# First layer of a two-block model: the keys' scale on ScalarE, and a new order of key transposes, first scores and value pairs

## The chip, the cores and the metric

The kernel runs on one core of one Trainium2 chip. The metric is the device time of one execution in microseconds (us): the median of several executions. A core has five engines with a queue each, worked off in order: TensorE (matmuls), VectorE, ScalarE, GpSimd and SyncE (which here only issues DMAs). Engines wait for one another by semaphores. In the profile they are called PE (PEld is TensorE's loading of the stationary operand), DVE, ACT, POOL and SP.

## The reference

A sequence of 256 tokens of width 1024 goes through two layers of a first block and one layer of a second, in float32. Only the mixer of the first layer is touched here. It projects the normed input and splits it in parts for a state-space mixer, a gated unit and differential attention:

```python
xn = rms_norm(h, attn_norm_g[layer])
proj = xn @ w_in[layer]
u_ssm, u_g, v_g, q, k, v = jnp.split(proj, [o1, o2, o3, o4, o5], axis=-1)
...
q = rms_norm(q, q_gain)          # 4 heads x 2 halves of 64
k = rms_norm(k, k_gain)
q = apply_rope(q, cos, sin)
k = apply_rope(k, cos, sin)
...
s = jnp.einsum("bqhcd,bkhcd->bhcqk", qb, k).astype(jnp.float32) * scale
s = jnp.where(mask, s, -jnp.inf)
p = jax.nn.softmax(s, axis=-1)
w = (p[:, :, 0] - lam * p[:, :, 1]).astype(v.dtype)
return jnp.einsum("bhqk,bkhe->bqhe", w, v)
```

The norm of a key is one factor for each token and each of the 8 half heads. The kernel turns the keys first and multiplies by that factor (held in `hr[:, 1, 8 * t + g]`, token tile t, half head g) afterwards: this multiplication is the keys' scale.

## The kernel before

**Weights.** All weights come in a stream of pairs of 128x1024 float32, 512 KB each. SyncE loads a pair into one of 7 raw buffers. ScalarE copies it to a rounded high part (`hi_upto`, line 1065, 6 buffers), VectorE subtracts to get a low part (`lo_upto`, line 1644, 7 buffers), and TensorE makes three products for each (high by high, high by low, low by high; lines 575 to 577 in `pair_products`). `hi_upto(n)` and `lo_upto(n)` do all pairs below n that aren't done yet; they stand by hand between the other work of their engine, which fixes the order. A high part waits until TensorE has used the pair 6 before it, a low part waits for its high part, and TensorE waits for both.

In layer 0 the pairs are numbered: q 0 to 3, k 4 to 7, state-space input 8 and 9, gates (`gmlp0`) 10 to 13, v 14 to 17, and then the output projection. The 256 tokens are two tiles of 128, so the three products of a pair make 12 matmuls (2 blocks of 128 rows, 2 tiles).

**TensorE in the stretch that the change touches** (lines 823 to 853), in layer 0: the transposes of the turned queries, the state-space input's shuffle and products (`input_products`), gate pairs 10 and 11, the transposes of the scaled keys (`head_transposes(1, ...)`, line 727), gate pairs 12 and 13, the scores of batch 0 (`scores(0)`: a mask product, line 741, and 16 small ones, line 744), v pairs 14 and 15, the Toeplitz products (line 650), v pair 16, the scores of batch 1, the spatial gating's products, v pair 17, the transposes of batch 0's probabilities, the scores of batch 2, and then the state-space output products (`output_products`, line 686).

**VectorE there**, layer 0: turns the keys (`rotary`), prepares the phase table (lines 341 to 343), low part 12, the keys' scale (line 1854, one operation over 128x1024), a memset (line 1858), low part 13, the rotation of the state-space inputs (`rotate`, lines 1781, 1782, 1785, 1786: two products from PSUM with a table, two sums), low part 14, the row maxima of the scores of batch 0 (`batch_max(0)`, lines 1796 and 1799), the small `lambdas`, low parts 15 and 16, the scans (line 1871), low part 17, `gate_rows`, `combine(0)`, low part 18, `states`, low part 19, and `batch_max(1)`.

**ScalarE there**, layer 0: high parts 15 and 16, the phase tables (lines 352 to 357), copies of the transposed keys out of PSUM (lines 1174, 1175), high part 17, the gates' squares (line 1182), high part 18, the exponentials of batch 0 (line 1207), the Toeplitz blocks' copies (line 1109), high part 19, the exponentials of batch 1, high part 20, the copy of the transposed probabilities (line 1215).

**GpSimd there**: the keys' inverse root (lines 1472, 1473, semaphore `hr_ready`), then six products of 128x1024 for the state-space output powers (lines 383 to 385, twice).

Of the kernel before, what the change touches and what calls it, by code (L numbers as in the profile page):

```python
# [21 lines left out]
TOK, TT = 256, 2  # L22
# [4 lines left out]
QKD, VD, DH = 64, 128, 4  # L27
# [11 lines left out]
ALU, ACT, AX = mybir.AluOpType, mybir.ActivationFunctionType, mybir.AxisListType  # L39
# [97 lines left out]
def build(nc, weights, x, mem, cols, rows, lams, bmerge, consts, amask, bexp, cexp, wst, wglu, out):  # L137
    with ExitStack() as ctx:
# [5 lines left out]
        def sem(name):  # L144
            if name not in sems:
                sems[name] = ctx.enter_context(nc.semaphore(name))
            return sems[name]
# [51 lines left out]
        def wide(ap, n, dim=1):  # L199

            a = ap.unsqueeze(dim)
            shape = list(a.shape)
            shape[dim] = n
            return a.to_broadcast(shape)
# [140 lines left out]
        def phase_tables(act, l):  # L345

            f, k = phase_scratch(l)
            co, si = (etab[:, i, :, :].rearrange("p s c -> p (s c)") for i in range(2))
            act.wait_ge(sem("turns_ready"), l + 1)
            if l:  # L350
                act.wait_ge(sem("states_ready"), 2 * l)
            act.activation(k, f, ACT.Sin, scale=-3.1415925).then_inc(sem("etab_ready"), 1)
            act.activation(si, f, ACT.Sin, scale=-6.283185).then_inc(sem("etab_ready"), 1)
            act.wait_ge(sem("etab_ready"), 4 * l + 1)
            act.activation(k, k, ACT.Square, scale=math.sqrt(2.0)).then_inc(sem("etab_ready"), 1)
            act.wait_ge(sem("etab_ready"), 4 * l + 3)
            act.activation(co, k, ACT.Identity, scale=-1.0, bias=1.0).then_inc(sem("etab_ready"), 1)
# [156 lines left out]
        def _(pe):  # L514
# [67 lines left out]
            def project(name, fm=False, xh=xth, xl=xtl, ready=None, pairs=None, order=None, half=None):  # L582

                c = chunk(name)
                _, n_k, cw = CHUNKS[c]
                banks = [PJ[BUF[c]][:, 0, :], PJ[BUF[c]][:, 1, :]]
                per = 1024 // cw
                for j in (range(PAIRS[c]) if pairs is None else pairs):  # L590
                    if j == 0:
                        emptied(name)
                    if ready:
                        pe.wait_ge(ready[0], ready[1] + (j + 1) * ready[2])
                    m = pair_products(SLOT[name, j], (order[j] if order else j) * per, banks, fm, xh, xl, cw,
                                      j == 0, j == PAIRS[c] - 1, half)
                    m.then_inc(pair_used, 1)
# [58 lines left out]
            for l in range(LAYERS):  # L656
# [61 lines left out]
                def head_transposes(which, banks):  # L718

                    if which == 0:  # L720
                        pe.wait_ge(sem("q_rot"), 2 * (l + 1))
                    else:
                        pe.wait_ge(sem("k_scaled"), l + 1)
                    for h in range(DH):
                        for t in range(TT):
                            o = banks[h // 2][:, (h % 2) * TOK + t * P:(h % 2) * TOK + (t + 1) * P]
                            m = pe.transpose(o, xn[:, t, which * 512 + h * P:which * 512 + (h + 1) * P], ident)
                    m.then_inc(sem("qk_tr"), 1)

                def scores(b):  # L730

                    t, heads = DB[b]
                    n = P * (t + 1)
                    if b == 0:
                        pe.wait_ge(sem("qk_ev"), 4 * (l + 1))
                    if b == 1:
                        pe.wait_ge(sem("w_used"), 2 * (l + 1))
                    if b == 2:
                        pe.wait_ge(sem("da_exp"), 16 * l + EXPS[0])
                    for c, bank in enumerate(DBANKS[b]):  # L740
                        pe.matmul(bank[:, :], identb[:, :], maskb[:, t, :], start=True, stop=False, skip_group_check=True)
                    for i, h in enumerate(heads):
                        for c, bank in enumerate(DBANKS[b]):
                            m = pe.matmul(bank[:, i * n:(i + 1) * n], qT[c * QKD:(c + 1) * QKD, h, t * P:(t + 1) * P],
                                          kT[c * QKD:(c + 1) * QKD, h, 0:n], start=False, stop=True, skip_group_check=True)
                    m.then_inc(sem("da_sc"), 1)
# [81 lines left out]
                if l == 0:  # L828
                    shuffle_in()
                    input_products()  # L830
                    project("gmlp0", pairs=[0, 1])
                    head_transposes(1, (S0, S1))
                else:
                    project(f"gmlp{l}", pairs=[0])
                    shuffle_in()
                    project(f"gmlp{l}", pairs=[1])
                    head_transposes(1, (S0, S1))
                    input_products()
                project(f"gmlp{l}", pairs=[2, 3])
                if l == 0:  # L840
                    pe.wait_ge(sem("maskb_ready"), 3)
                scores(0)
                if l == 0:
                    project("v0", pairs=[0, 1])
                    pe.wait_ge(sem("w_used"), 2)
                    for b in range(2):
                        toeplitz_products(0, b, (T0, T1)[b])
                    project("v0", pairs=[2])
                    pe.wait_ge(sem("mt_ready"), 8)
                    scores(1)  # L850
                    sgu_products()
                    project("v0", pairs=[3])
                    prob_transposes(0)
                else:
                    project(f"v{l}", pairs=[0])
                    scores(1)
                    project(f"v{l}", pairs=[1])
                    sgu_products()
                    project(f"v{l}", pairs=[2])
                    prob_transposes(0)  # L860
                    project(f"v{l}", pairs=[3])
# [193 lines left out]
        def _(act):  # L1055
# [81 lines left out]
            for l in range(LAYERS):  # L1137
# [32 lines left out]
                hi_upto(s0 + 17)  # L1170
                if l == 0:
                    phase_tables(act, 0)
                act.wait_ge(sem("qk_tr"), 2 * l + 2)
                act.copy(kT[:, 0:2, :], S0[:, :]).then_inc(sem("qk_ev"), 1)
                act.copy(kT[:, 2:4, :], S1[:, :]).then_inc(sem("qk_ev"), 1)
# [452 lines left out]
        def _(dve):  # L1628
# [122 lines left out]
            for l in range(LAYERS):  # L1751
# [6 lines left out]
                def heads8(ap):  # L1758
                    return ap.rearrange("p t (g d) -> p t g d", g=8)
# [89 lines left out]
                if l == 0:  # L1849
                    phase_turns(dve, link, 0)  # L1850
                    lo_upto(s0 + 13)
                dve.wait_ge(sem("hr_ready"), 2 * l + 2)
                k8 = heads8(xn[:, :, 512:1024])
                dve.tensor_tensor(k8, k8, wide(hr[:, 1, :].rearrange("p (t g) -> p t g", t=TT), QKD, 3), ALU.mult)\
                   .then_inc(sem("k_scaled"), 1)
                if l == 0:
                    dve.wait_ge(sem("mixw_landed"), 32)
                    dve.memset(wsts[64:128, :, 0:64], 0.0).then_inc(sem("wst_ready"), 1)
# [29 lines left out]
                if l:  # L1888
                    lo_upto(s0 + 18)
                    scans()  # L1890
                    batch_max(0)
                    lo_upto(s0 + 19)
                    gate_rows()
                    states()
                    lo_upto(s0 + 20)
                    dve.wait_ge(sem("states_ready"), 2 * (l + 1))
                    combine(0)
                    batch_max(1)
                else:
                    lo_upto(s0 + 15)  # L1900
                    batch_max(0)
                    lambdas()
                    lo_upto(s0 + 17)
                    scans()
                    lo_upto(s0 + 18)
                    gate_rows()
                    dve.wait_ge(sem("par_a"), 6)
                    for k in range(LAYERS):
                        link(dve.tensor_tensor(nlam[:, k:k + 1], lamv[:, 6 + k:7 + k], lamv[:, 2 + k:3 + k], ALU.subtract))
                        link(dve.tensor_scalar(nlam[:, k:k + 1], nlam[:, k:k + 1], -LAMBDA_INIT[k], None, ALU.add))  # L1910
                    combine(0)
                    lo_upto(s0 + 19)
                    states()
                    lo_upto(s0 + 20)
                    batch_max(1)
                    dve.wait_ge(sem("states_ready"), 2)
                    for k in range(LAYERS):
                        link(dve.tensor_scalar(row("sub", VD * k, VD), row("sub", VD * k, VD), math.sqrt(VD) * (1.0 - LAMBDA_INIT[k]),
                                               None, ALU.mult))
# [416 lines left out]
```

## Time and profile before

| | |
|---|---|
| Median of 3 executions | 1042.14 us (1041.73 to 1047.3) |
| The profiled execution | 1040.72 us, span 1038.9 us |
| TensorE busy | 1000.9 us (96%), 6106 matmuls |
| VectorE busy | 695.3 us (67%) |
| ScalarE busy | 547.9 us (53%) |
| GpSimd busy | 246.6 us (24%) |
| Mean granted clock of TensorE | 0.997 of full |

The span is the time from the first to the last recorded instruction; the execution's own time is 1.8 us longer. The busy shares are means over the whole program; the change touches the stretch from about 50 to 100 us of it. Times in the rows below are counted from the span's start. In the timelines a row is one instruction or several alike (x4), with its start and its duration; in brackets stands how long the engine was idle before it and what it waited for.

### The profile page before, as it was taken

How to read it: one execution, taken by the hardware profiler on the slowest of the kernel's cores; microseconds unless marked ns; L12 is line 12 of the kernel's file. 1: busy time of each engine (PE TensorE's matmuls, PEld its weight loads, DVE VectorE, ACT ScalarE, POOL GpSimd, SP SyncE). 2: the span in 40 equal slices, each digit the busy share in tenths (PEclk: the TensorE clock that was granted, in tenths of full speed). 3: DMA queues.
4: the chain of work that ended last, by engine and by line, in shares of the span. 5: the costliest groups of instructions: out<-in, count | busy, mean ns of one | idle time of the engine just before them, and what ended most of it. 6: DMA issues, size and time to landing. Idle time of an engine off the chain costs nothing.

```text
span 1038.9 us, 15870 instructions
## 1 busy us (share of the span) xinstructions
PE 1000.9 (96%) x6106; PEld 871.1 (84%) x6110; DVE 695.3 (67%) x1084; ACT 547.9 (53%) x910; POOL 246.6 (24%) x196
## 2 busy tenths in 40 slices
PE   5979999999999999999999999999999999999997
PEld 4858889999888888799999889877777888888775
DVE  6998567799854776577787653665665555445694
ACT  7656456557744656356665554544444553454532
POOL 4880103787200110104443000011212100000030
PEclk9999999999999999999999999999999999999999
DMA  8531355555555542555555555655444446434452
GB/s 291 197 102 61 116 177 176 183 177 182 187 185 162 168 134 64 165 186 184 183 182 184 184 175 188 191 167 173 133 134 138 143 145 200 141 113 132 142 162 81
DMA packets 48474, 165.96 MB, mean 160 GB/s; under 512 B 6544, under 2 KB 7056, under 8 KB 48400
## 3 DMA queue, kind: packets, MB, share of 16 engines
q1 hardware_dynamic: 48400, 164.95, 49.9%
q8 instruction: 49, 0.80, 0.3%
q14 instruction: 25, 0.20, 0.1%
HBM read 162.83 MB, written 1.05 MB: 158 GB/s over the span
## 4 chain that ended last, share of the span: by engine, by line
PE 83%; DVE 11%; ACT 3%; issue 2%; POOL 1%; DMA 1%; SPq 0%; DVEq 0%; POOLq 0%; ACTq 0%
PE PJ L575 13%; PE PJ L577 13%; PE PJ L576 13%; PE PJ L568 9%; PE PJ L570 9%; PE PJ L569 9%; DVE wlo L1644 3%; PE PJ L531 2%; PE PJ L533 2%; PE PJ L532 2%; PE T L996 1%; PE S L921 1%; PE S L976 1%; PE T L941 1%; PE T L987 1%
## 5 line engine op out<-in xcount | busy, mean ns | idle before, releaser
L1644 DVE TENSOR_TENSOR wlo<-raw,whi 128x1024 fp32r<-128x1024 f32 x294 | 377.5, 1314 | 155.4 <-ACT whi L1065 154.8
L1065 ACT ACTIVATE whi<-raw 128x1024 fp32r<-128x1024 f32 x294 | 303.8, 1063 | 71.4 <-DMA raw<-weights_in 65.3
L568 PE MATMUL PJ<-xth,whi 128*128 128x256 f32 x768 | 217.9, 284 | 2.0 <-DVE wlo L1644 1.2
L569 PE MATMUL PJ<-xtl,whi 128*128 128x256 f32 x768 | 217.3, 283 | 0.0
L570 PE MATMUL PJ<-xth,wlo 128*128 128x256 f32 x768 | 217.3, 283 | 0.0
L575 PE MATMUL PJ<-whi,xth 128*128 128x512 f32 (+1 forms) x480 | 193.8, 404 | 7.0 <-DVE wlo L1644 5.0
L577 PE MATMUL PJ<-whi,xtl 128*128 128x512 f32 (+1 forms) x480 | 186.9, 389 | 0.0
L576 PE MATMUL PJ<-wlo,xth 128*128 128x512 f32 (+1 forms) x480 | 185.9, 387 | 0.0
L568 PEld LDWEIGHTS PJ<-xth,whi 128*128 128x128 f32 x768 | 147.4, 192 | 3.3 <-issue 3.2
L569 PEld LDWEIGHTS PJ<-xtl,whi 128*128 128x128 f32 x768 | 147.4, 192 | 0.1
L570 PEld LDWEIGHTS PJ<-xth,wlo 128*128 128x128 f32 x768 | 147.4, 192 | 0.0
L1569 POOL TENSOR_TENSOR gtd<-acc 128x512 f32<-128x512 f32 x22 | 82.0, 3726 | 153.0 <-ACT acc L1291 149.7
L575 PEld LDWEIGHTS PJ<-whi,xth 128*128 128x128 f32 x480 | 90.7, 189 | 25.7 <-issue 6.6
L577 PEld LDWEIGHTS PJ<-whi,xtl 128*128 128x128 f32 x480 | 90.5, 189 | 19.6
L1983 DVE SCALAR_TENSOR_TENSOR acc<-PJ,colv,acc 128x255 f32<-128x255 f32 (+1 forms) x176 | 72.2, 474 | 48.8 <-ACT acc L1286 48.1
L576 PEld LDWEIGHTS PJ<-wlo,xth 128*128 128x128 f32 x480 | 90.9, 189 | 16.4
L1286 ACT ACTIVATE acc<-PJ,colv 128x256 f32<-128x256 f32 x88 | 42.5, 564 | 100.4 <-PE PJ L570 100.4
L575 PE MATMUL PJ<-whi,hth 128*128 128x512 f32 x144 | 57.2, 397 | 0.2 <-ACT whi L1065 0.2
L577 PE MATMUL PJ<-whi,htl 128*128 128x512 f32 x144 | 57.1, 396 | 0.0
L576 PE MATMUL PJ<-wlo,hth 128*128 128x512 f32 x144 | 57.1, 396 | 0.0
L1623 POOL TENSOR_TENSOR merged<-merged,gt 128x512 f32<-128x512 f32 x6 | 10.6, 1787 | 179.1 <-DVE gt L2179 179.1
L1406 ACT ACTIVATE sm<-S,sx 128x256 f32<-128x256 f32 x24 | 11.4, 475 | 56.6 <-DVE sx L2117 56.6
(395 smaller groups left out, 1433.0 us busy)
## 6 DMA issues: line engine op xcount, KB each, us to landing
raw<-weights_in SPq DMA_DIRECT2D x294, 512.0 KB, 3.5
rt<-bmerge_in SPq DMA_DIRECT2D x6, 256.0 KB, 4.1
xres<-x_in SPq DMA_DIRECT2D x2, 512.0 KB, 5.4
xn<-mem_in SPq DMA_DIRECT2D x2, 512.0 KB, 5.6
y_out<-xn SPq DMA_DIRECT2D x4, 256.0 KB, 2.4
rowv<-rows_in SPq DMA_DIRECT2D x1, 576.0 KB, 10.9
ptmp<-bexp_in SPq DMA_DIRECT2D x2, 256.0 KB, 6.1
cex<-cexp_in SPq DMA_DIRECT2D x2, 256.0 KB, 8.4
```

What stands on the lines that cost most here:

```text
L531: pe.matmul(o, h, wh, start=(j == 0 and kk == 0), stop=False, skip_group_check=True)
L568: pe.matmul(o, a, xh[:, k, :], start=(first and f % 2 == 0), stop=False, skip_group_check=True)
L569: pe.matmul(o, a, xl[:, k, :], start=False, stop=False, skip_group_check=True)
L570: m = pe.matmul(o, b, xh[:, k, :], start=False, stop=last, skip_group_check=True)
L575: pe.matmul(o, h, wh, start=first, stop=False, skip_group_check=True)
L576: pe.matmul(o, h, wl, start=False, stop=False, skip_group_check=True)
L577: m = pe.matmul(o, lw, wh, start=False, stop=last, skip_group_check=True)
L1065: act.activation(whi[:, p % HIGHS, :], raw[:, p % LOADS, :], ACT.Copy).then_inc(hi_ready, 1)
L1286: act.activation(acc[:, j % 2, i, :], PJ[BUF[c]][:, i // 2, (i % 2) * TOK:(i % 2 + 1) * TOK], ACT.Identity, scale=colv[:, k + 2:k + 3], bi ...
L1569: pool.tensor_tensor(gtd[:, j % 2, :, :], acc[:, j % 2, 0:2, :], acc[:, j % 2, 2:4, :], ALU.mult).then_inc(sem("gated"), 1)
L1644: dve.tensor_tensor(wlo[:, p % LOADS, :], raw[:, p % LOADS, :], whi[:, p % HIGHS, :].bitcast(F32), ALU.subtract).then_inc(lo_ready, 1)
L1983: dve.scalar_tensor_tensor(out=acc[:, j % 2, i, sh:TOK], in0=PJ[BUF[c]][:, i // 2, (i % 2) * TOK:(i % 2 + 1) * TOK - sh], scalar=colv[:, k ...
```

## The change

In layer 0 only:

- VectorE no longer scales the keys. ScalarE does, behind the phase tables, in 16 copies of 128x64 with a scale for each partition (two token tiles, eight half heads), in place, and does high part 17 right behind them.
- TensorE runs all four gate pairs (10 to 13) before the keys' transposes; then v pair 14, the scores of batch 0, v pair 15, and the rest as before.
- VectorE does low part 15 ahead of the row maxima of batch 0, rather than behind them.

Layer 1's order stays. Its wait for the scaled keys counts 16 signals of layer 0 instead of one.

```diff
--- before.py
+++ after.py
@@ -720,7 +720,7 @@
                     if which == 0:
                         pe.wait_ge(sem("q_rot"), 2 * (l + 1))
                     else:
-                        pe.wait_ge(sem("k_scaled"), l + 1)
+                        pe.wait_ge(sem("k_scaled"), 16 + l)
                     for h in range(DH):
                         for t in range(TT):
                             o = banks[h // 2][:, (h % 2) * TOK + t * P:(h % 2) * TOK + (t + 1) * P]
@@ -828,20 +828,21 @@
                 if l == 0:
                     shuffle_in()
                     input_products()
-                    project("gmlp0", pairs=[0, 1])
+                    project("gmlp0")
                     head_transposes(1, (S0, S1))
+                    project("v0", pairs=[0])
+                    pe.wait_ge(sem("maskb_ready"), 3)
+                    scores(0)
+                    project("v0", pairs=[1])
                 else:
                     project(f"gmlp{l}", pairs=[0])
                     shuffle_in()
                     project(f"gmlp{l}", pairs=[1])
                     head_transposes(1, (S0, S1))
                     input_products()
-                project(f"gmlp{l}", pairs=[2, 3])
+                    project(f"gmlp{l}", pairs=[2, 3])
+                    scores(0)
                 if l == 0:
-                    pe.wait_ge(sem("maskb_ready"), 3)
-                scores(0)
-                if l == 0:
-                    project("v0", pairs=[0, 1])
                     pe.wait_ge(sem("w_used"), 2)
                     for b in range(2):
                         toeplitz_products(0, b, (T0, T1)[b])
@@ -1170,6 +1171,13 @@
                 hi_upto(s0 + 17)
                 if l == 0:
                     phase_tables(act, 0)
+                    act.wait_ge(sem("k_rot"), 2)
+                    act.wait_ge(sem("hr_ready"), 2)
+                    for t in range(TT):
+                        for g in range(8):
+                            part = xn[:, t, 512 + QKD * g:512 + QKD * g + QKD]
+                            act.activation(part, part, ACT.Copy, scale=hr[:, 1, 8 * t + g:8 * t + g + 1]).then_inc(sem("k_scaled"), 1)
+                    hi_upto(s0 + 18)
                 act.wait_ge(sem("qk_tr"), 2 * l + 2)
                 act.copy(kT[:, 0:2, :], S0[:, :]).then_inc(sem("qk_ev"), 1)
                 act.copy(kT[:, 2:4, :], S1[:, :]).then_inc(sem("qk_ev"), 1)
@@ -1849,10 +1857,11 @@
                 if l == 0:
                     phase_turns(dve, link, 0)
                     lo_upto(s0 + 13)
-                dve.wait_ge(sem("hr_ready"), 2 * l + 2)
-                k8 = heads8(xn[:, :, 512:1024])
-                dve.tensor_tensor(k8, k8, wide(hr[:, 1, :].rearrange("p (t g) -> p t g", t=TT), QKD, 3), ALU.mult)\
-                   .then_inc(sem("k_scaled"), 1)
+                if l:
+                    dve.wait_ge(sem("hr_ready"), 2 * l + 2)
+                    k8 = heads8(xn[:, :, 512:1024])
+                    dve.tensor_tensor(k8, k8, wide(hr[:, 1, :].rearrange("p (t g) -> p t g", t=TT), QKD, 3), ALU.mult)\
+                       .then_inc(sem("k_scaled"), 1)
                 if l == 0:
                     dve.wait_ge(sem("mixw_landed"), 32)
                     dve.memset(wsts[64:128, :, 0:64], 0.0).then_inc(sem("wst_ready"), 1)
@@ -1897,7 +1906,7 @@
                     combine(0)
                     batch_max(1)
                 else:
-                    lo_upto(s0 + 15)
+                    lo_upto(s0 + 16)
                     batch_max(0)
                     lambdas()
                     lo_upto(s0 + 17)
```

## Rows read from the trace of the kernel before

**Rows 1.** the chain of waits, 40 to 130 us (start, duration in us, what)

```profile
68.13 2.90 DVE wlo L1644
...
90.21 0.70 DVE st_ L1796
...
94.99 1.97 PE PJ L686 x16
```

**Rows 2.** grouped waits of TensorE, 40 to 130 us (total us, times, longest)

```profile
PE PJ L575 <- DVE wlo L1644: 5.0, 2, 3.1
PE S L727 <- DVE xn L1854: 1.8, 1, 1.8
```

**Rows 3.** busy us per engine, 50 stretches of 0.5 us, 60 to 85

```profile
sum 25.00, PE 19.95 PEld 16.48 DVE 24.31 ACT 11.81 POOL 16.21; mean PE 0.40 PEld 0.33 DVE 0.49 ACT 0.24 POOL 0.32
```

**Rows 4.** timeline of VectorE (start, us, engine, line, operation, out<-in)

```profile
55.72 1.22 DVE L1644 TENSOR_TENSOR wlo<-raw,whi 128x1024 fp32r<-128x1024 f32 x1
56.85 3.00 DVE L1854 TENSOR_TENSOR xn<-xn,hr 128x1024 f32<-128x1024 f32 x1
...
60.26 2.50 DVE L1644 TENSOR_TENSOR wlo<-raw,whi 128x1024 fp32r<-128x1024 f32 x1
62.68 1.22 DVE L1781 TENSOR_TENSOR qh<-T,etab 128x1024 f32<-128x1024 f32 x1
...
65.06 0.69 DVE L1785 TENSOR_TENSOR sw<-qh 128x512 f32<-128x512 f32 x1
65.67 2.46 DVE L1786 TENSOR_TENSOR sw<-qh 128x512 f32<-128x512 f32 x1
68.05 2.98 DVE L1644 TENSOR_TENSOR wlo<-raw,whi 128x1024 fp32r<-128x1024 f32 x1
...
72.39 0.92 DVE L1799 SCALAR_TENSOR_TENSOR st_<-st_,hr 128x8 f32<-128x8 f32 x1
...
74.60 2.36 DVE L1644 TENSOR_TENSOR wlo<-raw,whi 128x1024 fp32r<-128x1024 f32 x2
```

**Rows 5.** timeline of GpSimd, its six power products of layer 0

```profile
56.03 2.73 POOL L383 TENSOR_TENSOR gpw<-gpw,apw 128x1024 f32<-128x1024 f32 x1
58.73 2.95 POOL L384 TENSOR_TENSOR ptmp<-gpw,apw 128x1024 f32<-128x1024 f32 x1
61.76 3.28 POOL L385 TENSOR_TENSOR gpw<-gpw,ptmp 128x1024 f32<-128x1024 f32 x1
65.11 2.47 POOL L383 TENSOR_TENSOR gpw<-gpw,apw 128x1024 f32<-128x1024 f32 x1
67.54 2.41 POOL L384 TENSOR_TENSOR ptmp<-gpw,apw 128x1024 f32<-128x1024 f32 x1
70.02 3.26 POOL L385 TENSOR_TENSOR gpw<-gpw,ptmp 128x1024 f32<-128x1024 f32 x1
```

**Rows 6.** timeline of TensorE, from the gate pairs to pair 15

```profile
52.42 0.47 PE L575 MATMUL PJ<-whi,xth 128*128 128x512 f32 x1
...
57.76 0.39 PE L577 MATMUL PJ<-whi,xtl 128*128 128x512 f32 x1
...
66.86 1.16 PE L744 MATMUL S<-kT,qT 64*128 64x128 f32 x16
71.17 0.47 PE L575 MATMUL PJ<-whi,xth 128*128 128x512 f32 x1 [3.15 <-DVE wlo L1644]
...
75.97 0.47 PE L575 MATMUL PJ<-whi,xth 128*128 128x512 f32 x1 [1.83 <-DVE wlo L1644]
```

**Rows 7.** two of those stretches (busy us and count by engine, then TensorE's granted clock)

```profile
76.50:77.00 0.50, 0.50 (x3) 0.39 (x2) 0.50 (x2) 0.50 (x4) 0.00 (x0) 0.59 0.92 377
...
80.00:80.50 0.50, 0.50 (x5) 0.42 (x4) 0.50 (x1) 0.00 (x0) 0.00 (x0) 0.99 0.00 0
```

**Rows 8.** timeline of ScalarE, a norm copy early on and the last phase table

```profile
10.36 2.15 ACT L1085 ACTIVATE xth<-S,colv 128x128 fp32r<-128x128 f32 x8
...
58.18 0.63 ACT L357 ACTIVATE etab<-md 128x512 f32<-128x512 f32 x1
```

## The prediction

> **What bounds the kernel now.** I read the chain of waits first, because TensorE is busy 96% of the span and only the places where it isn't can be shortened. From 40 to 91 us that chain isn't on TensorE at all: it stays on VectorE, through the low part of weight pair 14 [rows 1] down to the row maxima of the second batch of scores [rows 1]; it then goes over ScalarE (the exponentials of batch 1, a weight copy, the copy of the first transposed probabilities), and reaches TensorE at 94.99, where the output products wait for that copy [rows 1]. After that TensorE has work to the end of the layer. So whatever moves VectorE's row maxima of batch 1 moves the whole rest of the program by the same amount. The second view, the grouped waits of TensorE, says what it lacks in this stretch: 5.0 us in two waits for low parts (pairs 14 and 15) and 1.8 us for the scaled keys [rows 2]. The change takes aim at the 1.8 and moves the 5.0. In the third view, the busy time of stretches, VectorE is busy 24.31 of 25 us from 60 to 85, TensorE 19.95 [rows 3]: VectorE is the queue that is full, and TensorE's waits are what it looks like from the other side.
>
> Two things in the timelines decide the size. VectorE's operations here don't take their own time. The key scale takes 3.00 us, the low part of pair 13 takes 2.50, the second rotation sum 2.46 where the first of the same shape takes 0.69, and pair 14's low part 2.98, against 1.18 for each of two later ones of the same shape [rows 4]. Laid beside GpSimd's six power products [rows 5], each of the long ones ends about 1.1 us (0.6 for the short shape) after a GpSimd product ends: 58.76 to 59.85, 61.68 to 62.76, 67.58 to 68.13, 69.95 to 71.03. GpSimd in turn waits for each of them: 58.73 plus 2.95 is 1.82 after 59.85. So the two take turns whenever VectorE reads two SBUF operands. The two rotation products, which read one operand from PSUM, take 1.2 us under a running GpSimd product [rows 4] and don't wait. GpSimd's own pieces between turns are 1.8, 1.8 and 2.3 us, twice over. The second thing is TensorE's clock: after 3.15 us idle, 2.9 us of work and 1.83 us idle it fell to the lower of its two levels (1.2 GHz) inside pair 15 [rows 6, 7], and its matmuls start 0.43 us apart instead of 0.23.
>
> **The change, part by part.** Removed from VectorE in layer 0: one key scale. It holds 3.00 us, of which 1.9 is the wait for GpSimd and 1.1 is work [rows 4, 5]. What matters is who takes its turn. Put in order with the new queue:
> - Low part 13 now follows pair 12's directly, waits for GpSimd's product that ends at 58.76, and ends at 59.86. It has taken the key scale's place.
> - The two rotation products (PSUM operand, 1.13 us each, start to start) run to 62.1. GpSimd meanwhile does its next piece to 61.68 and starts the 2.3 us one, unhindered, to 64.04.
> - The first rotation sum reads two SBUF operands, and waits from 62.2 to 64.04; today it starts at 65.06 and finds GpSimd between two products. It ends at 64.65. GpSimd, already waiting, takes 1.82 (66.47), the second sum 0.6 (67.05), GpSimd 1.82 (68.87), low part 14 ends at 69.95.
> - Today low part 14 ends at 71.03. Of the 3.00 us removed, 1.1 us is left: the work, not the wait.
>
> Added to ScalarE: 16 copies of 128x64 with a scale per partition, behind the phase tables that end at 58.81 [rows 8]. The trace has no such shape. From above, the nearest form with a scale operand is the 128x128 norm copy, 8 in 2.15 us or 0.27 each [rows 8], which gives 4.3 us; from below, half of that, 2.1. I take 0.2 each, 3.2 us, to 62.0, near the upper row since little of a short copy is elements. The Trainium skill, page "ScalarE: Activation LUTs", section "Step-by-step: what each stage is for", would make it 0.24 each, 3.8 us (fixed cost with one pointer operand plus 0.833 ns an element, less the overlap). All of these cost nothing, as does the high part of pair 17 behind them: TensorE asks for the keys only when pair 13 is through. 24 matmuls of pairs 10 and 11 span 52.42 to 57.76, 0.232 us apart [rows 6], so all four gate pairs now run from 52.42 to 63.6, with the low parts of pairs 12 and 13 there at 56.94 [rows 4] and 59.86. The 1.8 us wait is gone. If the cover went (copies over 0.28 each) the transposes would start late, and still have until 70.
>
> What is late next is pair 14. TensorE has done the eight transposes at 64.6 (1 us for them, an estimate from 16 smaller products in 1.16 [rows 6]), and then nothing until low part 14 lands: idle 64.6 to 70.1. One long gap of 5.5 us has replaced gaps of 1.8 and 3.15 us.
>
> Moved: the first scores behind pair 14. They take 1.7 us after the last matmul before them (mask product and 16 small products, the latter starting at 66.86 and taking 1.16 [rows 6]). At the upper clock pair 14 ends at 72.85 and the scores at 74.55. Moved too: low part 15 ahead of the first row maxima. It waits for GpSimd's last product (69.95 plus 2.3) and ends at 73.4, so VectorE stands idle 1.2 us for the scores. The maxima then end, with their small product, at 76.15; today that is 73.31, with 0.75 us of it a last wait for GpSimd [rows 4]. That is 2.85 us later, and low part 15 (1.14, half of the pair at 74.60) no longer stands behind it: 1.7 us later for all that follows on VectorE. Nothing behind it has slack in that queue, so the maxima of batch 1, the exponentials, the high part and the output products go 1.7 us later. The pairs 15 and 16, which TensorE does earlier, gain nothing: it arrives at the output products early and waits there.
>
> **The clock** is the unknown. TensorE will be idle 5.5 us before pair 14, and again some 5 us before the output products. Neither gap is in the trace. From below it costs nothing: after the 3.15 us alone the level had stayed up. From above, the one fall in this stretch lasts from the slice at 76.50, where the mean is 0.59, to about 80.0 [rows 7], 3.4 us at half speed, 1.7 us of work lost if TensorE works all through it. I take 1.4 for each gap, near the upper end, since both are longer than the ones that brought that fall, and off it, since a part of the low stretch can lie in the gap. The Trainium skill, page "TensorE: Matmul & The Clock Gate", section "What's actually happening", says that the throttled state is the default and that activity releases it; the trace agrees, falling after sparse work [rows 7]. This speaks against gathering two short waits into one long one. Sum: +1.7 +1.4 +1.4 = +4.5 us. The profiled execution, 1040.72 us, becomes 1045.2. Its runs' median is 1042.14, 1.4 higher, which gives 1046.6; I say 1045.9, between the two.
>
> **Rivals.**
> - The turns with GpSimd don't recur, and the queue is simply shorter: the first rotation sum runs at 62.2, low part 14 ends at 64.6, scores end at 69.2, 1.8 us before today's maxima begin; the 0.75 wait goes and low part 15's 1.14 is out of the way: -3.7, 1037 to 1038.5. For it: a GpSimd span is rough. Against it: four long VectorE operations and four matching ends. The point from which it decides: the first rotation sum starting its work before 63.
> - No clock fall, or one: +1.7 to +3.1, 1042.4 to 1045.2.
> - The clock stays low through pair 14, the scores and the output products: instead of 1.4 the first costs 4.4 (2.75 + 1.7 at half speed), and the second 3.5. +9.6, 1050.3 to 1051.7: clearly slower. Against it: with work going on, the level was back by 80.0, some 4 us after the work of pair 15 began.
> - The keys' scale on ScalarE holds up TensorE after all, over 0.7 us a copy: then the kernel transposes later than 70 and the loss grows by the excess. Nothing in rows near this shape speaks for it.
>
> **How the numbers follow.** Forecast 0.52 (its own range 1044 to 1047.8); turns gone 0.13; one fall or none 0.17; long fall 0.13; the rest 0.05. The range 1039 to 1049.8 leaves out most of the gain below and the long fall above. 0.5%, about what a measurement of this kernel tells from no change, is 5.2 us: 1036.9 and 1047.4. Slower by more: the long fall and the top quarter of the forecast, 0.13 + 0.12 = 0.25. Faster by more: the far end of the first rival, 0.05. Within: 0.70.
>
> **What would show it.** Right: the wait of the key transposes is gone; one wait of about 5.5 us for low part 14 before pair 14; the first rotation sum on VectorE spans some 2.4 us in place of 0.69; VectorE idle for the first scores at about 73.4 to 76; the first small product of the maxima ended at 76 to 77.6 in place of 73.31; output products near 98 in place of 94.99; the granted clock at half just after 70 and again near 98. Wrong: low part 14 done before 66, or output products before 95.

## The result: 0.7% slower, and where the time went

The changed kernel takes 1052.08 us (median of 7, 1050.87 to 1055.11). The kernel before, run again beside it, takes 1046.82 (median of 7, 1041.62 to 1048.56). The ratio is 1.0069, 95% interval 1.0043 to 1.0096: slower. The means of the two sevens lie 7.2 us apart (1052.45 and 1045.21), the medians 5.3; why they differ, experiment 3 shows. The forecast was 1045.9 with a range to 1049.8, so the time lies outside it. The first lines of the page, of the changed kernel's profiled execution (1053.52 us), and the granted clock in 40 slices of the span:

```profile
span 1051.7 us, 15886 instructions
...
PE 1010.4 (96%) x6106; PEld 880.5 (84%) x6110; DVE 694.9 (66%) x1083; ACT 551.8 (52%) x926; POOL 246.6 (23%) x196
...
PEclk9988899999999999999999999999999999999999
```

The span is 12.8 us longer than in the profile before. The clock's row has three eights where it had only nines: TensorE's clock was at its lower level (1.2 GHz) for parts of the stretch from 53 to 131 us. TensorE's grouped waits from 40 to 130 us (total, times, longest) answer to [rows 2]:

```profile
PE PJ L575 <- DVE wlo L1652: 5.7, 1, 5.7
PE PJ L686 <- ACT pT L1223: 5.2, 1, 5.2
```

The 1.8 us for the scaled keys is gone. In its place stand one wait of 5.7 us for low part 14 and one of 5.2 us for the copy of the probabilities, ahead of the output products. The same in VectorE's timeline (start, duration; line numbers are 8 to 9 higher than before), which answers to [rows 4]:

```profile
57.03 2.52 DVE L1652 TENSOR_TENSOR wlo<-raw,whi 128x1024 fp32r<-128x1024 f32 x1
...
61.85 2.58 DVE L1793 TENSOR_TENSOR sw<-qh 128x512 f32<-128x512 f32 x1
64.35 2.44 DVE L1794 TENSOR_TENSOR sw<-qh 128x512 f32<-128x512 f32 x1
66.72 6.28 DVE L1652 TENSOR_TENSOR wlo<-raw,whi 128x1024 fp32r<-128x1024 f32 x2
77.02 1.42 DVE L1804 TENSOR_REDUCE st_<-S 128x4 f32<-128x512 f32 x2 [4.02 <-PE S L744]
```

Low part 13 (57.03) takes 2.52 us: it has the key scale's place. The first rotation sum (61.85) takes 2.58 in place of 0.69, the second 2.44, the two low parts 6.28 together, and then VectorE is idle 4.02 us for the scores. GpSimd's products in the same stretch, against [rows 5]:

```profile
61.48 2.40 POOL L385 TENSOR_TENSOR gpw<-gpw,ptmp 128x1024 f32<-128x1024 f32 x1
63.96 2.29 POOL L383 TENSOR_TENSOR gpw<-gpw,apw 128x1024 f32<-128x1024 f32 x1
```

The turns are those of the forecast: 61.48 plus 2.40 ends at 63.88, and the first sum 0.55 later; 63.96 plus 2.29 ends at 66.25, and the second sum at 66.79. Low part 14, the first of the two in the row at 66.72, takes 2.98 us and ends at 69.70 (forecast 69.95). ScalarE's part, against [rows 8]:

```profile
58.38 3.92 ACT L1179 ACTIVATE xn<-xn,hr 128x64 f32<-128x64 f32 x16
```

The 16 copies take 0.24 us each and end at 62.3, ahead of TensorE's transposes, as cheap as they were forecast. The prediction's sentence on the Trainium skill, page "ScalarE: Activation LUTs", gave 0.24 us each as well; the fixed cost and the overlap that it uses stand there in the section "What ACT_TABLE_LOAD costs", behind the one it names. And TensorE, against [rows 6]; first pair 14, the scores, the output products, then the powers' products (line 692) and the shuffle behind them (line 703):

```profile
63.09 1.03 PE L727 MATMUL S<-cst,xn 128*128 128x128 f32 x8
69.84 0.77 PE L575 MATMUL PJ<-whi,xth 128*128 128x512 f32 x1 [5.72 <-DVE wlo L1652]
...
75.81 1.16 PE L744 MATMUL S<-kT,qT 64*128 64x128 f32 x16
...
99.20 3.65 PE L686 MATMUL PJ<-uc,mT 128*128 128x64 f32 x16 [5.20 <-ACT pT L1223]
...
103.49 6.93 PE L692 MATMUL PJ<-sw,gpw 128*128 128x63 f32 x32
...
113.02 2.46 PE L703 MATMUL PJ<-uT,cst 128*32 128x128 f32 x32
```

Two of these rows in the kernel before:

```profile
97.29 3.68 PE L692 MATMUL PJ<-sw,gpw 128*128 128x63 f32 x32
...
102.29 2.46 PE L703 MATMUL PJ<-uT,cst 128*32 128x128 f32 x32
```

From the output products' start to the shuffle's, the same 64 matmuls take 13.8 us (99.20 to 113.02) and took 7.3 (94.99 to 102.29). The windows say why. Columns: stretch, its length, busy us and count of PE, PEld, DVE, ACT, POOL, then the granted clock, the busy share of the DMA engines and GB/s:

```profile
66.00:68.00 2.00, 0.00 (x0) 0.00 (x0) 2.00 (x2) 1.97 (x5) 2.00 (x2) 1.00 0.08 33
68.00:70.00 2.00, 0.16 (x1) 0.19 (x2) 2.00 (x2) 0.58 (x1) 1.92 (x2) 0.66 0.00 0
...
96.00:98.00 2.00, 0.00 (x0) 0.00 (x0) 0.00 (x0) 2.00 (x7) 0.00 (x0) 0.50 0.00 0
```

```profile
69.84:75.30 5.46, 5.46 (x12) 3.99 (x14) 3.16 (x1) 0.00 (x0) 3.72 (x3) 0.50 0.00 2
99.20:113.00 13.80, 13.80 (x64) 13.48 (x64) 7.26 (x15) 6.89 (x10) 0.00 (x0) 0.50 0.00 1
```

and for the same matmuls before:

```profile
94.99:102.20 7.21, 7.21 (x64) 7.13 (x64) 7.07 (x15) 5.87 (x9) 0.00 (x0) 1.00 0.08 32
```

The clock falls after 68, more than 4 us into the first gap, and pair 14 runs at half speed from its first to its last matmul. It falls again in the second gap, before 96, and stays down for all of the output products, although TensorE is busy 13.80 of 13.80 us there. It is back at 1.00 from 76 us, behind pair 14, and from 113 us, at the shuffle.

To compare kernels whose starts differ by some tenths, the times below are counted from the start of low part 12, the last operation that all have in common. "Start" is from there to the output products; "length" is from the output products to the shuffle behind them; "to the norm" is from low part 12 to the transposes of the next norm, the end of the stretch. These three are of the one profiled execution, the medians and ratios of all.

| kernel | start | length | to the norm | median us | ratio to before (95%) |
|---|---|---|---|---|---|
| before, profile shown above | 39.3 | 7.3 | 77.5 | | |
| before, another execution | 39.3 | 12.7 | 83.9 | 1046 to 1047 | 1 |
| changed | 43.8 | 13.8 | 88.6 | 1052.08 | 1.0069 (1.0043 to 1.0096) |
| changed, first gap filled | 41.2 | 13.8 | 86.4 | 1050.91 | 1.0062 (1.0041 to 1.0083) |
| changed, second gap filled | 42.5 | 7.3 | 80.8 | 1046.09 | 1.0004 (0.9985 to 1.0024) |
| changed, both filled | 41.2 | 7.3 | 79.5 | 1042.76 | 0.9973 (0.9954 to 0.9992) |
| both filled (the first with 20 transposes, not 46), GpSimd's last products held back | 40.7 | 7.3 | 78.9 | 1041.61 | 0.9968 (0.9951 to 0.9985) |
| scores first | 38.2 | 13.2 | 83.0 | 1045.35 | 1.0001 (0.9978 to 1.0024) |
| scores first, filled | 38.3 | 7.3 | 76.5 | 1041.25 | 0.9952 (0.9935 to 0.9970) |
| before, early gaps filled | 39.3 | 13.8 | 84.0 | 1046.73 | 0.9988 (0.9968 to 1.0008) |
| before, last gap filled | 39.2 | 7.3 | 77.5 | 1042.19 | 0.9977 (0.9957 to 0.9997) |
| scale on ScalarE alone | 41.0 | 12.0 | 84.1 | 1048.42 | 1.0028 (1.0009 to 1.0047) |
| order alone | 45.1 | 13.8 | 90.0 | 1052.74 | 1.0085 (1.0059 to 1.0111) |

The ratios come from four comparisons, each with its own executions of the kernel before (medians 1046.82, 1046.98, 1047.23 and 1046.48), so small differences between ratios of different comparisons mean little. One execution of the kernel before, 1411.27 us at a mean granted clock of 0.656, is left out of them as a slow run. The last rows of the stretch, for the kernel before in its two executions and for the changed kernel:

```profile
133.25 0.63 PE L622 MATMUL S<-cst,xn 128*128 128x128 f32 x4 [0.41 <-DVE xn L1653]
...
138.82 0.63 PE L622 MATMUL S<-cst,xn 128*128 128x128 f32 x4 [0.41 <-DVE xn L1653]
...
144.02 0.63 PE L622 MATMUL S<-cst,xn 128*128 128x128 f32 x4 [0.41 <-DVE xn L1661]
```

### The profile page after: what moved, and what is told of

Read it like the earlier page. It is cut to its first block, busy times and chain, and to the rows that moved or that the text cites. A ratio compares the mean times of both kernels' runs of the same rounds, so it can differ in the third digit from the quotient of the medians.

```text
span 1051.7 us, 15886 instructions
## 1 busy us (share of the span) xinstructions
PE 1010.4 (96%) x6106; PEld 880.5 (84%) x6110; DVE 694.9 (66%) x1083; ACT 551.8 (52%) x926; POOL 246.6 (23%) x196
## 4 chain that ended last, share of the span: by engine, by line
PE 81%; DVE 12%; ACT 3%; issue 2%; POOL 1%; DMA 1%; SPq 0%; DVEq 0%; POOLq 0%; ACTq 0%
PE PJ L575 13%; PE PJ L577 12%; PE PJ L576 12%; PE PJ L568 9%; PE PJ L569 9%; PE PJ L570 9%; DVE wlo L1652 3%; PE PJ L531 2%; PE PJ L533 2%; PE PJ L532 2%; PE T L997 1%; PE PJ L692 1%; DMA raw<-weights_in 1%; PE S L977 1%; PE S L922 1%
## 5 line engine op out<-in xcount | busy, mean ns | idle before, releaser
L576 PE MATMUL PJ<-wlo,hth 128*128 128x512 f32 x144 | 57.1, 396 | 0.0
L577 PE MATMUL PJ<-whi,htl 128*128 128x512 f32 x144 | 57.1, 396 | 0.0
```

The source lines that it names most:

```text
L576: pe.matmul(o, h, wl, start=False, stop=False, skip_group_check=True)
L577: m = pe.matmul(o, lw, wh, start=False, stop=last, skip_group_check=True)
```

## The experiments

**1. The gaps filled, one at a time.** Each filling is a number of transposes of a constant into a bank whose contents nobody reads, placed where TensorE stands idle. The kernel before already does this elsewhere: behind the first transposes of the next norm it has 14 such transposes (`keep_busy`, line 602, at 134.15 us). The two edits, which run alone and together:

```diff
                     head_transposes(1, (S0, S1))
+                    emptied("v0")
+                    keep_busy(A[:, 0, :], 46)
                     project("v0", pairs=[0])
...
                     prob_transposes(0)
+                    pe.wait_ge(sem("da_exp"), EXPS[0])
+                    keep_busy(S0, 44)
```

First gap alone, expected: 

> The changed kernel, with 46 transposes into the still empty bank of the value projection placed in TensorE's first gap (64.0 to 69.8 in its trace). Nothing waits for them and they should end before low part 14 is there. Theory A (the clock falls because TensorE stands idle, and that is what the change costs beyond the queue): pair 14 runs at the upper clock, 2.8 us in place of 5.3, the first scores end near 74.4 and the output products start near 96.6 in place of 99.2; the second gap and its long low stretch stay. Span near 2.6 us under the changed kernel's, ratio to before about 1.005. Theory B (pair 14 and the output products are slow for another reason, such as operands or DMA traffic): no gain, or a loss, since the transposes only load TensorE.

Second gap alone: 

> The changed kernel, with 44 transposes into a free score bank ahead of the scores of batch 2, to fill TensorE's second gap (94.0 to 99.2). Theory A: the first low stretch stays, the output products still start at 99.2, but take 5.9 us to the value products as before the change, not 11.0; about 5 to 6.6 us less than the changed kernel, ratio to before about 1.002 to 1.004. Theory B: still 11 us from the output products to the value products.

Both: 

> The changed kernel with both gaps filled. Theory A: what is left is the queue of VectorE alone, output products near 96.7 in place of 94.99 before the change, +1.7 us, ratio about 1.0016, the clock at its upper level from 20 us on. Theory B: as the changed kernel, 1.007.

Measured, first gap filled (its own 46 transposes, pair 14, the scores, the output products):

```profile
64.17 5.18 PE L602 MATMUL PJ<-cst 128*128 128x128 f32 x46
70.02 0.47 PE L575 MATMUL PJ<-whi,xth 128*128 128x512 f32 x1 [0.66 <-DVE wlo L1654]
...
73.36 1.16 PE L744 MATMUL S<-kT,qT 64*128 64x128 f32 x16
...
96.75 3.65 PE L686 MATMUL PJ<-uc,mT 128*128 128x64 f32 x16 [5.23 <-ACT pT L1225]
```

Counted from low part 12, pair 14 starts when it did, and the scores and the output products 2.6 us earlier; pair 14 ran at the upper clock, and the output products are as slow as in the changed kernel. Second gap filled:

```profile
91.00 4.97 PE L602 MATMUL S<-cst 128*128 128x128 f32 x44
...
97.89 1.97 PE L686 MATMUL PJ<-uc,mT 128*128 128x64 f32 x16 [0.43 <-ACT pT L1225]
...
100.19 3.68 PE L692 MATMUL PJ<-sw,gpw 128*128 128x63 f32 x32
```

The output products take 1.97 in place of 3.65 us, the powers' products 3.68 in place of 6.93. Both filled (the output products alone):

```profile
96.24 1.97 PE L686 MATMUL PJ<-uc,mT 128*128 128x64 f32 x16 [0.43 <-ACT pT L1227]
```

Theory A holds in all three, and Theory B falls: with 46 and 44 transposes more on TensorE the changed kernel takes 1042.76 us in place of 1052.08. In the profiled executions the second fall costs 6.5 us (length 13.8 against 7.3) and 1.9 us of pure queue are left (41.2 against 39.3; forecast 1.7).

The first fall has no such fixed size. It costs 2.6 us from the changed kernel to the one with the first gap filled (43.8 to 41.2), but only 1.3 between the two kernels whose second gap is filled (42.5 to 41.2): in the first of these the clock was back at 1.00 from 73 us, inside pair 14, and not from 76. So the output products of that run started 1.3 us earlier than I expected. The medians are 1.2 us apart in the one case (1052.08 and 1050.91, two ratios whose intervals overlap) and 3.3 in the other (1046.09 and 1042.76). That the first gap costs something rests on the profiles and on this second pair; its size stays open between about 1 and 3 us.

One more expectation was off: both filled, I expected 1.0016 and measured 0.9973. The queue's 1.9 us is there, but the kernel before isn't what I took it for; that is experiment 3.

**2. The scores first.** The series pair 14, scores, maxima is undone, which takes two moves back together, the scores' on TensorE and low part 15's on VectorE:

```diff
                     head_transposes(1, (S0, S1))
-                    project("v0", pairs=[0])
                     pe.wait_ge(sem("maskb_ready"), 3)
                     scores(0)
-                    project("v0", pairs=[1])
+                    project("v0", pairs=[0, 1])
...
-                    lo_upto(s0 + 16)
+                    lo_upto(s0 + 15)
                     batch_max(0)
```

> The changed kernel with the first scores back ahead of value pair 14, and low part 15 back behind the first row maxima; the keys' scale stays on ScalarE and all four gate pairs ahead of the transposes. Queue theory (the row maxima wait for low part 14, its pair and then the scores, which the changed order put in series): scores end at 67, maxima start at 69.8 right behind low part 14, output products near 93.7, 1.3 us before the unchanged kernel's; TensorE's gap before pair 14 is 3 us, so the clock may hold there. Ratio about 0.9985 to 1.000. Rival (the loss comes from the scale on ScalarE or from the gate pairs' place): ratio stays near 1.007.

```profile
69.30 0.47 PE L575 MATMUL PJ<-whi,xth 128*128 128x512 f32 x1 [2.74 <-DVE wlo L1651]
...
93.10 3.03 PE L686 MATMUL PJ<-uc,mT 128*128 128x64 f32 x16 [2.00 <-ACT pT L1222]
```

The start is 38.2, 1.0 us under the kernel before (expected 1.3): the whole loss in the queue came from putting the scores behind pair 14, with low part 15 ahead of the maxima, and the rest of the change is worth 1.0 us. But TensorE now waits 2.00 us ahead of the output products, and in this execution the clock fell within a microsecond of their start (0.89 from 93 to 94 us, 0.50 after that). The ratio is 1.0001. Two of the 12 executions took 1040.2 and 1040.7 us, the other ten 1045.2 to 1047.4; the two weren't profiled.

**3. What the kernel before is.** Its times lie in two groups: of 29 executions in one comparison, nine at 1040.1 to 1042.0, and twenty at 1046.3 to 1048.0. In two other comparisons the lower group has ten of 34 and four of 23 (in the first of these, three more lie between the groups, at 1044.7 to 1045.1). The three that stood ahead of the prediction were two of the first and one of the second, and the profile was of the first.

> The kernel before, unchanged, for another profile. Its times lie in two groups, ten of 35 at 1040.0 to 1041.8 and most others at 1046.5 to 1048.4, and the profile of before is one of the lower group. Theory A: an execution of the upper group shows the clock at its lower level through the output products and on (about 95 to 110 us), 11 us to the value products in place of 5.9, with nothing else changed. Rival: it is slower elsewhere (DMA, or spread over the whole span).

The second such run had the same expectation: 

> The kernel before once more, with the same expectation, to have a better chance of an execution of the upper group.

Both came out in the upper group (1046.84 and 1046.89 us), with the same picture (pairs 14 and 15, output products, powers' products):

```profile
70.35 0.47 PE L575 MATMUL PJ<-whi,xth 128*128 128x512 f32 x1 [3.17 <-DVE wlo L1644]
...
75.12 0.47 PE L575 MATMUL PJ<-whi,xth 128*128 128x512 f32 x1 [0.31 <-DVE wlo L1644]
...
94.14 2.50 PE L686 MATMUL PJ<-uc,mT 128*128 128x64 f32 x16 [2.00 <-ACT pT L1215]
...
97.29 6.93 PE L692 MATMUL PJ<-sw,gpw 128*128 128x63 f32 x32
...
106.82 3.48 PE L703 MATMUL PJ<-uT,cst 128*32 128x128 f32 x32
```

This is the unchanged kernel with the second fall: TensorE waits 2.00 us ahead of the output products, and the clock falls some 1.3 us after they have begun (1.00 from 94 to 95 us, 0.70 from 95 to 96, then 0.50). It is back only inside the shuffle, which takes 3.48 us in place of 2.46. So the column "length" misses a part of this fall. To the norm it costs 6.4 us (83.9 against 77.5), as much as in the changed kernel. The value products come 9.9 us after the output products' start, where I had expected 11; it was 5.8 in the profile ahead of the prediction. In these two executions the clock also fell inside pair 14 (0.75 from 71 to 72 us, then 0.50), which ended before low part 15 was there and cost nothing. In the profile ahead of the prediction it had fallen inside pair 15 [rows 7] instead. Pair 15 then took longer, which cost nothing, TensorE reached the output products 1.6 us later, waited 0.4 us, and the clock stayed up. The fall at 76.5, which I had used only to price a fall, had closed the costly gap. That reading rests on three profiles, one of the lower group and two of the upper; experiment 4 tests the gap itself.

**4. Which gap of the kernel before does it.** Two fillings were run, of the early gaps (22 transposes ahead of pair 14, 14 ahead of pair 15) or of the last one (16 ahead of the scores of batch 2):

> The kernel before with its two gaps ahead of pairs 14 and 15 filled: 22 transposes into the empty value bank, 14 into a free bank. Theory A: no fall at 76, and none of the upper group: all executions near 1040 to 1042, ratio to before about 0.995. Rival (the two groups have another cause): the two groups stay.

```profile
68.89 2.62 PE L602 MATMUL PJ<-cst 128*128 128x128 f32 x22
...
95.96 3.58 PE L686 MATMUL PJ<-uc,mT 128*128 128x64 f32 x16 [2.02 <-ACT pT L1220]
...
100.18 6.93 PE L692 MATMUL PJ<-sw,gpw 128*128 128x63 f32 x32
```

Wrong: three of its 12 executions are at 1041.4 to 1042.0, the others at 1044.9 to 1049.7. Filling the early gaps kept the clock at 1.00 through pairs 14 and 15, and left the 2.0 us gap where it was. What spared the three isn't known, since none of them was profiled; a gap of 2 us is not followed by the costly fall every time. The other filling:

> The kernel before with only its last gap filled, the one of up to 2.0 us ahead of the output products: 16 transposes ahead of the scores of batch 2. The gaps ahead of pairs 14 and 15 stay. Theory A (that short gap brings the long low stretch of the upper group, and the output products can't bring the clock back themselves): only the lower group is left, 1040 to 1043, ratio to before about 0.995. Rival (the earlier gaps bring it): two groups as before, ratio 1.000.

```profile
90.67 1.91 PE L602 MATMUL S<-cst 128*128 128x128 f32 x16
...
94.31 1.97 PE L686 MATMUL PJ<-uc,mT 128*128 128x64 f32 x16 [0.23 <-ACT pT L1217]
```

All 12 executions lie between 1040.1 and 1043.5, ratio 0.9977 (0.9957 to 0.9997). None is of the upper group: the 2 us ahead of the output products make it. The ratio is less far down than I expected (0.995).

**5. The best of both.** The scores first, with the fillings of experiment 4 (22, 14 and 16):

> The scores-first order (keys' scale on ScalarE, four gate pairs, transposes, first scores, value pairs) with its gaps filled: 22 and 14 transposes ahead of pairs 14 and 15, 16 ahead of the scores of batch 2. Theory A: output products at about 93, no low stretch, some 1 to 1.9 us under the filled kernel before: 1039 to 1041, ratio to before about 0.994. Rival (the output products stay slow since they are narrow): 1045 as without the fillings.

```profile
93.49 1.97 PE L686 MATMUL PJ<-uc,mT 128*128 128x64 f32 x16 [0.24 <-ACT pT L1229]
```

1041.25 us, ratio 0.9952 (0.9935 to 0.9970). It beats the kernel before and the changed one. Against the kernel before with the last gap filled it starts the output products 1.0 us earlier, and the medians are 0.9 us apart (1042.19 and 1041.25); but the two come from different comparisons and their intervals overlap, so that advantage isn't shown in the time.

**6. The turns.** Here GpSimd's second set of products waits for low part 14. Both gaps are filled, the first with 20 transposes in place of 46 (that edit isn't shown below):

```diff
             output_powers(pool, link, 0, 0, ptmp)
+            pool.wait_ge(lo_ready, 15)
             output_powers(pool, link, 0, 1, ptmp)
```

> The changed kernel with both gaps filled, and GpSimd's last three power products held back until low part 14 is done. Theory of the turns (VectorE's two-operand operations and GpSimd's products exclude each other): the second rotation sum takes 0.7 in place of 2.45 us, low part 14 takes 1.2 in place of 3.0 and is done near 66.3 in place of 69.8, and the products then make the operations behind it wait instead (low part 15, the small product of the first maxima up to about 73.3). Output products near 94, ratio to before about 0.995 or a little less. Rival (those operations are slow on their own): low part 14 still near 69.8, and the time of the filled kernel, 0.9973.

```profile
61.34 1.22 DVE L1794 TENSOR_TENSOR qh<-T,etab 128x1024 f32<-128x1024 f32 x1 [2.34 <-ACT etab L357]
...
64.34 0.68 DVE L1799 TENSOR_TENSOR sw<-qh 128x512 f32<-128x512 f32 x1
64.94 2.35 DVE L1657 TENSOR_TENSOR wlo<-raw,whi 128x1024 fp32r<-128x1024 f32 x2
```

With GpSimd silent the second sum takes 0.68 us and both low parts 2.35 together, against 2.44 and 6.28. That VectorE's two-operand operations are long because of GpSimd's products, and not on their own, is shown. The gain at the end is not: start 40.7 and not near 39. TensorE's rows show two reasons:

```profile
66.67 2.35 PE L602 MATMUL PJ<-cst 128*128 128x128 f32 x20
68.78 0.48 PE L575 MATMUL PJ<-whi,xth 128*128 128x512 f32 x1
```

First, TensorE's clock was at its lower level from 50.4 to 57.1 us in this execution, and the keys' transposes came 3.2 us later than in the changed kernel (65.80, counted from low part 12). Second, low part 14 was done at 66.16, but the 20 idle transposes stood ahead of pair 14 and held it to 68.78. Here the filling itself cost about 2.1 us, an estimate from these two rows; without it the start would be near 38.6. VectorE waited 6.1 us for the scores. What the held-back products would gain with a filling that fits wasn't run.

**7. The two parts alone.**

> One part alone: the keys' scale on ScalarE, TensorE and VectorE otherwise in the order of before. The 16 copies end near 62.2, so the transposes come 2.3 us later, TensorE is idle 4.3 us ahead of them, low part 14 is ready at 69.8 and the scores end near 70.5. Maxima about 0.9 us earlier than before, output products near 94.1. The gap ahead of them is 2 to 3 us, so the long low stretch comes in every execution: about the upper group of before, 1046 to 1048, ratio 1.000 to 1.002.

```profile
62.13 1.97 PE L727 MATMUL S<-cst,xn 128*128 128x128 f32 x8 [4.53 <-ACT xn L1179]
...
96.15 1.97 PE L686 MATMUL PJ<-uc,mT 128*128 128x64 f32 x16 [1.98 <-ACT pT L1223]
```

> The other part alone: TensorE's and VectorE's new order, the keys' scale still one operation on VectorE. Low part 14 comes at 71.0 in place of 69.8, and the series of its pair, the scores and the maxima stays. If the order is what costs, output products near 100, both low stretches, ratio about 1.008; if the scale on ScalarE is what costs, ratio near 1.000.

```profile
70.25 0.77 PE L575 MATMUL PJ<-whi,xth 128*128 128x512 f32 x1 [2.81 <-DVE wlo L1645]
...
99.85 3.65 PE L686 MATMUL PJ<-uc,mT 128*128 128x64 f32 x16 [5.24 <-ACT pT L1216]
```

The order alone costs more than the whole change (start 45.1 against 43.8): the cost is the order's. The scale alone I had 2.6 us too early: TensorE, idle 4.5 us ahead of the transposes, ran them and most of the gate pairs behind at the lower clock (8 transposes in 1.97 us, 1.03 at the upper one; granted clock 0.50 from 61 to 67 us). The second fall comes 2.1 us after the output products have begun, so they take 1.97 us and the powers' products behind them 6.92. It was to come in every execution; one of the 12 took 1042.83 us, the others 1045.9 to 1049.2. The fall ahead of the transposes is what experiment 1 showed, at a third place.

## Why the prediction was wrong

- **What bounds the kernel** was right: VectorE up to the maxima of batch 1, then ScalarE, then the output products. Moving that chain moved the end.
- **The turns with GpSimd**, and with them low part 14 at 69.95, were right: measured 69.70. So was the cost of the 16 copies, 0.2 us each against 0.24, and that they hide.
- **The queue's term, +1.7 us,** was right in mechanism and size: 1.9 us with both gaps filled. Experiments 2 and 7 show that it is the order's.
- **The clock's term, 1.4 us for each gap, failed.** It measured 2.6 us for the first gap (1.3 in another profile) and 6.5 us for the second. I had named 1.7 us as the most that a fall can cost, from the one fall in the trace, with TensorE back at the upper level by 80.0. That bound was not one. At pair 14 the low level held from before the pair to after it. At the output products it held through 13.8 us of unbroken work. My third rival, the long fall with +9.6 us, is what came: 1.9 + 2.6 + 6.5 = 11.0 us, and 10.8 are there between the two profiles by the end of the stretch (144.02 against 133.25 for the next norm's transposes). Its total came near, its parts didn't: it has 4.4 us for the first fall and 3.5 for the second. I had given it 0.13, for the reason that with work going on the level had come back.
- **The base failed too.** The sum was made on an execution of the lower group, and two of three times shown were of that group. Most executions of the kernel before already pay for the second fall, 6.4 us to the norm. Against them the changed kernel loses what they don't have, the queue's 1.9 us and the first fall's 2.6: 4.5 us, and 4.7 are there in the profiles (88.6 against 83.9 to the norm). The medians differ by 5.3. That this lies close to the +4.5 of the forecast is luck: two falls at 1.4 us were forecast on top of the queue, and one at 2.6 is left, because the other stands in both. The profile shown is another 2 us longer behind the stretch, between 700 and 720 us, where the granted clock of the changed kernel's execution is 0.91. The clock fell between 680 and 720 us in seven of the 14 profiles, of filled kernels too, and not in the others; why is open.
- One sentence of the part on the change, that TensorE's earlier pairs 15 and 16 gain nothing since it waits at the output products, was right for the queue and passed over what the wait costs. With the first gap filled TensorE reaches the output products 1.3 us earlier than in the upper group of before, and they can start 1.9 us later, so its wait grows from 2.0 to 5.2 us.

## What to carry to other kernels

Count TensorE's idle stretches as a cost of their own, even where another engine sets the time: an order that makes it arrive early at a wait can slow everything behind the wait. Take the price from the work that stands behind the gap, at half speed, and not from how long another fall lasted; where that work isn't in the trace at the lower level, carry the long fall as the upper bound. Before a profile is used as a base, see whether the times have groups, and of which one it is. A number of idle transposes into a free bank is a cheap test, and here a cheap cure, but it has to end before the operand comes: in experiment 6 it held up the pair behind it.

## What the hardware showed that I had not expected

- The same 64 matmuls, from the output products to the shuffle, ran at the lower level from the first to the last in the changed kernel (busy 13.80 of 13.80 us, granted clock 0.50) and at the upper level in the kernel before (busy 7.21 of 7.21 us, 1.00). Which level they ran at went with the idle time ahead of them. Of the 14 profiles, six had 0.2 or 0.4 us and kept the upper level; the eight others, with 2.0 or 5.2 us, ran wholly or mostly at the lower one. In the five with 2.0 us the level fell only when the work had begun, 0.1 to 2.1 us into it. The times of six unprofiled executions (three, two and one in experiments 4, 2 and 7) suggest that such a gap can also pass without a fall.
- A fall of the clock early on can make a kernel faster, by filling a later gap: the kernel before took 1041 us in the profile with the fall at pair 15, and 1047 in the two with it at pair 14.
- The turns of VectorE and GpSimd could be laid out ahead to a few tenths of a microsecond (low part 14 at 69.95, measured 69.70): a wait removed from one operation was passed to the next two-operand one.
